# HGRN2's chunk states behind the last level in place of ahead of the diagonal, diagonal and levels two to three k-tiles sooner

## The reference

```python
def hgrn2_chunked(q, k, v, g, S0, chunk):
    """HGRN2: S_t = diag(f_t) S_{t-1} + k_t v_t^T with k_t = 1 - f_t, g = log f_t, o_t = S_t^T q_t."""
    def step(S, xs):
        qc, kc, vc, gc = xs
        b = jnp.cumsum(gc, axis=-2)
        diff = b[..., :, None, :] - b[..., None, :, :]
        decay = jnp.exp(jnp.where(incl, diff, -jnp.inf))
        A = jnp.einsum('bhtk,bhsk,bhtsk->bhts', qc, kc, decay)
        o = (jnp.einsum('bhck,bhkv->bhcv', qc * jnp.exp(b), S)
             + jnp.einsum('bhts,bhsv->bhtv', A, vc))
        bl = b[..., -1:, :]
        S_new = (jnp.exp(bl[..., 0, :])[..., None] * S
                 + jnp.einsum('bhck,bhcv->bhkv', kc * jnp.exp(bl - b), vc))
        return S_new, o
```

## Time and profile before

| | us |
|---|---|
| median of 3 runs | 3001.03 (2996.76 to 3002.65) |
| the profiled execution, its own time | 3001.41 |
| its span in the trace | 2999.7 |
| PE busy | 2924.2 (97% of the span) |
| DVE busy | 2022.4 (67%) |
| ACT busy | 1190.8 (40%) |
| PE in the chain that ended last | 90% |
| mean granted clock of PE | 0.992 |

### The profile page before, as it was taken

The page is one execution under the profiler, slowest core; times in us unless marked ns, Lnnn a source line. Parts: engine busy times, 40 slices in busy tenths (PEclk is TensorE's granted clock), DMA queues, the critical chain, the costliest instruction groups (busy, mean ns, idle before and its releaser), DMA issues.

```text
span 2999.7 us, 52045 instructions
## 1 busy us (share of the span) xinstructions
PE 2924.2 (97%) x21800; PEld 2876.1 (96%) x21800; DVE 2022.4 (67%) x2796; ACT 1190.8 (40%) x1506; POOL 316.7 (11%) x432
## 2 busy tenths in 40 slices
PE   7999999999999999999989999999999999999998
PEld 7999999999999999989989999999999999999998
DVE  5556564746464747465477777777778788788885
ACT  4333333333333333333244444444444444444454
POOL 5111102020201011102100000000000000000111
PEclk9999999999999999999999999999999999999999
DMA  7334573333233424345334444544567666666665
GB/s 215 68 84 77 78 78 72 82 79 79 64 92 59 100 49 96 87 126 148 109 108 139 155 146 139 162 139 146 159 202 225 195 193 193 197 192 196 193 196 185
DMA packets 516473, 397.46 MB, mean 133 GB/s; under 512 B 16960, under 2 KB 484176, under 8 KB 516240
## 3 DMA queue, kind: packets, MB, share of 16 engines
q1 hardware_dynamic: 462272, 268.86, 36.3%
q0 software_dynamic: 22896, 88.43, 8.0%
q10 hardware_dynamic: 31072, 36.85, 4.1%
HBM read 309.72 MB, written 84.37 MB: 131 GB/s over the span
## 4 chain that ended last, share of the span: by engine, by line
PE 90%; DVE 5%; issue 2%; ACT 2%; DMA 1%; ACTq 0%; POOL 0%; SPq 0%; DVEq 0%; POOLq 0%
PE main L1279 39%; PE main L936 32%; PE mx L1279 7%; PE mx L1179 2%; PE mx L1012 1%; PE mx L1076 1%; PE mx L1084 1%; PE mx L996 1%; DVE w_lo L1825 1%; PE mx L1119 0%; ACT w_hi L1367 0%; PE mx L1055 0%; PE mx L1186 0%; PE mx L1196 0%; ACT tmp L1458 0%
## 5 line engine op out<-in xcount | busy, mean ns | idle before, releaser
L1279 PE MATMUL main<-forms_b,w_hi 128*128 128x288 f32 x3072 | 616.6, 296 | 10.8 <-DVE w_lo L2371 6.6
L936 PE MATMUL main<-h_hi,w_hi 128*128 128x296 f32 (+1 forms) x2592 | 612.0, 317 | 12.0 <-DVE w_lo L1825 12.0
L1279 PE MATMUL main<-forms_a,w_hi 128*128 128x288 f32 x3072 | 615.4, 296 | 5.8 <-DVE forms_a L2424 4.7
L936 PE MATMUL main<-h_lo,w_hi 128*128 128x296 f32 (+1 forms) x2592 | 564.6, 299 | 0.0
L936 PE MATMUL main<-h_hi,w_lo 128*128 128x296 f32 (+1 forms) x2592 | 564.1, 299 | 0.0
L1279 PEld LDWEIGHTS main<-forms_b,w_hi 128*128 128x128 f32 x3072 | 494.3, 189 | 12.2 <-DVE w_lo L2371 9.4
L1279 PEld LDWEIGHTS main<-forms_a,w_hi 128*128 128x128 f32 x3072 | 495.0, 189 | 6.9 <-issue 5.2
L1279 PE MATMUL main<-forms_a,w_lo 128*128 128x288 f32 x1536 | 455.2, 296 | 0.0
L1279 PE MATMUL main<-forms_b,w_lo 128*128 128x288 f32 x1536 | 453.4, 295 | 0.0
L936 PEld LDWEIGHTS main<-h_hi,w_hi 128*128 128x128 f32 x2592 | 414.8, 191 | 27.8 <-DVE w_lo L1825 17.4
L936 PEld LDWEIGHTS main<-h_lo,w_hi 128*128 128x128 f32 x2592 | 422.1, 189 | 0.0
(11 more groups left out here) (381 smaller groups left out, 3583.3 us busy)
## 6 DMA issues: line engine op xcount, KB each, us to landing
w_raw<-in_w_in SPq DMA_DIRECT2D x130, 512.0 KB, 8.1
w_raw<-in_w_up SPq DMA_DIRECT2D x128, 512.0 KB, 4.2
w_raw<-in_w_down SPq DMA_DIRECT2D x100, 512.0 KB, 4.4
u_forms<-ub POOLq DMA_DIRECT2D x32, 1152.0 KB, 6.8
z<-x_scratch SPq DMA_DIRECT2D x32, 576.0 KB, 7.4
x_scratch<-z POOLq DMA_DIRECT2D x31, 576.0 KB, 3.1
stage<-u_forms ACTq DMA_DIRECT2D x30, 576.0 KB, 4.0
w_raw<-in_w_out SPq DMA_DIRECT2D x32, 512.0 KB, 4.0
```

The lines of the kernel that those rows point to most:

```text
L936: ins = mm(out[:, half, :], w[:, ring, k, :], x[:, kx, half * width:half * width + width], start=first and n == 0, stop=last_ and n == 2)
L1279: ins = mm(out, w[:, k, :], x[:, kx, :], start=i in (0, 1, 3) and k == 0 and n == 0, stop=k == KP - 1 and n == 2, skip_group_check=True)
```

## The change

The stage `stw` is put behind `l64`, and `diag` and the levels move up. The table becomes: `turn_k` 18, `diag` 20, levels 22, 25, 29, 32, 36, 40, 43, `stw` 47, `o` 50. The steps in `HG_PE` and `HG_DVE` follow; `stw` on PE now waits for `a64` as well, `diag` for `kdt`, the first two levels for ACT's copy `vt` in place of `sc_4` (they use the PSUM banks that it reads), and `o` for `sc_4` in place of `a64`. No operation is added or removed.

```diff
--- before.py
+++ after.py
@@ -196,8 +196,8 @@
               **spread(["t1"] + T_STEPS + ["p64", "tp64", "vn0", "st0"]
                        + [f"{s}_{c}" for c in range(1, NW) for s in ("ws", "vn", "st")], 25, 57),
               "stb": 58, "out": 61}
-HG_STAGES = {"gates": 0, "conv_in": 5, "gates_b": 8, "turn_v": 10, "turn_k": 18, "stw": 20, "diag": 22,
-             **spread([f"l{b}" for b in LEVELS] + ["o", "out", "st0"], 24, 58)}
+HG_STAGES = {"gates": 0, "conv_in": 5, "gates_b": 8, "turn_v": 10, "turn_k": 18, "diag": 20,
+             **spread([f"l{b}" for b in LEVELS] + ["stw", "o", "out", "st0"], 22, 58)}
 
 START_PE = ["conv_rows", "vec_rows"] + [f"turn{k}" for k in range(KT)] + ["rstd", "cols"]
 START_ACT = ["ln", "exp", "a", "lb", "b_exp", "b_ln", "b_sig", "s_exp", "s_ln", "e_exp"]
@@ -213,13 +213,12 @@
            + ["tt64", "vx0", "vx", "sc_0", "o0"] + [f"{s}_{c}" for c in range(1, NW) for s in ("r", "sc")]
            + ["sb", "y1", "y"])
 GDN_POOL = [f"x{b}" for b in INV]
-HG_PE = ["turn_v", "turn_k", "stw", "diag"] + [f"l{b}" for b in LEVELS] + ["o0", "o", "out", "st0"]
+HG_PE = ["turn_v", "turn_k", "diag"] + [f"l{b}" for b in LEVELS] + ["stw", "o0", "o", "out", "st0"]
 HG_ACT = (["exp", "zexp", "ln", "lnlb", "sig", "zln", "zsig", "eb", "kdexp", "vt"] + [f"e{b}" for b in LEVELS]
           + ["o0", "o", "osq", "oln", "oexp"])
 LEVEL_DVE = [s for i, b in enumerate(LEVELS[1:]) for s in ([f"a{LEVELS[i]}", f"q{b}", f"kk{b}"] + ([f"arg{2 * b}"] if b < 64 else []))]
-HG_DVE = (["clamp", "zclamp", "g", "b", "k0", "k", "kdarg", "kd", "arg1", "vx", "kdt", "q1", "arg2", "sc_0"]
-          + [f"sc_{c}" for c in range(1, NW)] + ["diag", "qe", "zs"] + LEVEL_DVE + ["a64"]
-          + ["y1", "y", "sb_scale", "sb"])
+HG_DVE = (["clamp", "zclamp", "g", "b", "k0", "k", "kdarg", "kd", "arg1", "vx", "kdt", "q1", "arg2", "diag", "qe", "zs"]
+          + LEVEL_DVE + ["a64"] + [f"sc_{c}" for c in range(NW)] + ["y1", "y", "sb_scale", "sb"])
 HG_POOL = ["zero"]
 
 
@@ -1160,11 +1159,13 @@
                     W(hdve, "kdt")
                     W(hdve, "vx")
                     W(hact, "vt")
+                    W(hdve, "a64")
                     mm(bank(0, 0, P), hkdt[:, 0, :], hvx[:, SB, :], start=True, stop=True)
                     for c in range(1, NW):
                         ins = mm(mxf[:, P * c:P * c + P], hkdt[:, c, :], hvt[:, c, :], start=True, stop=True)
                     hpe.done(ins, "stw")
                 elif stage == "diag":
+                    W(hdve, "kdt")
                     for c in range(NW):
                         ins = mm(mxf[:, 1024 + P * c:1024 + P * c + P], win(hk, c), win(hq, c), start=True, stop=True)
                     hpe.done(ins, "diag")
@@ -1172,14 +1173,17 @@
                     b = int(stage[1:])
                     i = LEVELS.index(b)
                     W(hdve, f"kk{b}" if i else "q1")
-                    W(hdve, "sc_4" if i < 2 else f"a{LEVELS[i - 2]}")
+                    if i < 2:
+                        W(hact, "vt")
+                    else:
+                        W(hdve, f"a{LEVELS[i - 2]}")
                     n_ = 64 if b == 64 else P
                     for c in t_levels(b):
                         left = win(hkk if i else hk, c, n_)
                         ins = mm(bank(i % 2, 64 * c, 64, n_), left, hqq[:, ctok(c):ctok(c) + 64], start=True, stop=True)
                     hpe.done(ins, stage)
                 elif stage == "o":
-                    W(hdve, "a64")
+                    W(hdve, "sc_4")
                     W(hact, "eb")
                     pe.wait_ge(s_hst, h * 16 + 16)
                     for b in range(SB):
```

## The result

The changed kernel takes 3072.82 us (median of 3 runs, 3069.53 to 3077.55) where the kernel before takes 3001.03: a ratio of 1.0247, with an interval of 1.0233 to 1.026. The forecast was 3058, with a range from 3034 to 3071. The direction, the two waits and their places are as forecast; what they cost beyond themselves is not. The profiled execution of the changed kernel is the slowest of its three; the mean clocks of the others were 0.982 (3069.53 us) and 0.981 (3072.82).

What follows compares the result with a forecast made beforehand. PE was taken to bound the kernel, busy 2924.2 of 2999.7 us. Terms 38.2 + 17.3 + 2.1 - 0.3 - 0.6 = +56.7 us on the profiled 3001.41 gave 3058 us, range 3034 to 3071.

Steps and rivals of the forecast that it cites:

- Two waits at levels 2 and 8: In each of seven stretches PE reaches both levels before DVE's operands: 2.5 and 2.95 us, together +38.2 us.
- No wait at levels 4, 16, 32 and 64: Level 4 stays with room; levels 16, 32 and 64 have an estimated 0.5 to 1.7 us to spare.
- none at `o` in the stretches: At `o`, three k-tiles behind the states' products, the operand chain has 0.4 us to spare.
- The states themselves cost nothing: The states' products take PE 1.12 us, as much at the new place as at the old.
- The last head: States' products directly ahead of `o`: PE waits, +2.1 us; its wait at level 4 loses some 0.3 us.
- The clock: Half clock behind each level 8 wait and every second level 2 wait, 1.65 us each: +17.3 us, bounds 0 and 23.
- rival (2): Every wait costs the clock, also the last head's: 3066 us, or 3069 with a further stretch wait; chance 0.14.
- the start: First head: two columns' turns of the DeltaNet gates move from k-tile 24 to 22: -0.6 us.
- The rule on the clock: Only idle gaps longer than both level waits lower the clock: clock term 0, 3041 us; as rival, chance 0.14.

Runs made afterwards that it cites:

- shorter waits: The changed kernel with level 2 one k-tile later (26) and level 8 two later (34; later levels 38, 41, 44): 3030.76 us, ratio 1.0109.

## Why the prediction was right and wrong

**Two waits at levels 2 and 8: right.** Forecast as idle time 2.35 and 2.8, found 2.33 and 2.80, in each of the seven stretches, at the two places named, with the causes named: DVE's wait for ACT at `w_lo`, forecast at about 2.5 us, is 2.45 at 879.84, and the border of units 3 and 4 for level 8. Filling both (3039.74) shows their price by itself: 38.7 us between the medians, and 5.4 us in each of the clean heads, where the step had 38.2 and 5.45.

**No wait at levels 4, 16, 32 and 64: right**, and none at `o` in the stretches. The total of line L1183 is 37.2 in 16, and 7 x 5.13 + 1.3 = 37.2.

**The states themselves cost nothing: right** (1.0005 with them alone moved).

**The last head: right.** The wait at `o` is 1.92 us, forecast as about 1.9; the one at level 4 is 0.81 where it was 1.02. Rows of the changed kernel:

```profile
1391.13 1.33 PE L1183 MATMUL mx<-tmp 128*128 128x64 f32 x10 [0.81 <-DVE tmp L2069]
...
1421.99 1.95 PE L1190 MATMUL mx<-tmp,hstate 128*128 128x8 f32 x16 [1.92 <-DVE tmp L2137]
```

**The clock: the step that failed.** "I let each of its seven cost the clock ... I count every second. 7 x 1.5 x 1.65 = +17.3 us. The bounds are 0 and 14 x 1.65 = 23 us." Two things were wrong in it. In the changed kernel not every second but every wait of 2.33 us cost clock, so that 14 of 14 did; that is what rival (2) had. And one spell of about 3.3 us per wait, taken from one place of the MLP, was half of what followed: 6.8 us at 13 of them. The price of a piece was about right: 1.50 and 1.56 us in two experiments, against 1.65. In the profiled execution the term is 27 x 1.52 = 41 us, and between the medians, by the kernel with filled gaps, 33: both beyond the bound of 23. The windows from level 2 to level 2, of after and of before, show it in one row each: PE's busy time in the same 1151 or 1148 records is 159.82 against 153.22 us, and the clock 0.96 against 1.00.

```profile
882.61:1049.88 167.27, 159.82 (x1151) 154.68 (x1151) 90.50 (x162) 54.13 (x76) 21.10 (x28) 0.96 0.32 72
```

```profile
843.00:998.87 155.87, 153.22 (x1148) 148.22 (x1148) 89.78 (x161) 54.27 (x76) 20.86 (x28) 1.00 0.34 77
```

The row in the MLP was one sample of a thing that varies with its position, and I used it as a price. The trace of before had the longer spell too, at the last head's wait for `w_lo`:

```profile
1363.24 0.85 PE L936 MATMUL main<-h_hi,w_hi 128*128 128x288 f32 x2 [4.31 <-DVE w_lo L1825]
```

```profile
1361.00:1367.70 6.70, 4.46 (x18) 4.46 (x19) 3.98 (x5) 0.00 (x0) 1.05 (x2) 0.50 0.37 102
```

The prediction passed over it: it reads the 9s in the earlier trace rows as the full level in every slice. Two other terms partly covered the miss: the start was 2.1 us better where I had 0.6, and 2.4 us of small waits went that I had not counted.

**The range** had its top at 3071, 1.8 us below the result. It followed from "14 x 1.65", with an allowance for one more wait, and no allowance for a longer spell.

**The rule on the clock.** The forecast kept a rule of the Trainium skill as a rival. What the runs show: in the changed kernel all waits of 2.80 and 2.33 us came with a granted clock of 0.50, in the kernel with the levels alone 13 of 14, and so did five of seven of 1.51 us. The Trainium skill (TensorE: Matmul & The Clock Gate, HAM oscillation) has as its rule that only idle gaps longer than any of these do harm; by it this kernel would have taken 3041, as the forecast worked out, and the measurement decides against it. The same section tells of a kernel in which the loss is paid anew in each turn of the loop; with that this trace agrees, with 6.8 us behind both waits in six heads one after the other.

## What to carry to other kernels

In an order written by hand, an operation's place on the engine that uses it is only half of the change: read where its operand stands in the making engine's own queue, above all whether a wait for a third engine (here the rounding of weights) stands ahead of it. Where the operand can be made ahead of that, the earlier place costs nothing; the same look at the waits already in the table then gave 0.66%. Price a new wait of a nearly always busy PE at its length plus a loss of clock that can be as large again (here 38 and 41 us for the waits of 2.33 and 2.80 us; 1.5 us or nothing behind those of 1.51), and let the range reach from the loss in no turn to the longest spell in every turn: one wait of 14 in a kernel like this one cost no clock, and the wait of 1.51 us cost it in five heads and not in two.

## What the runs showed of the hardware

- The half clock came in pieces of 3.4 or 6.8 us here, and 3.4 us of it cost 1.50 (158.97 against 160.47) to 1.56 us (161.17 against 162.73). Which of the two followed went with how long after the wait the clock fell: 6.8 us where it fell from 0.5 us ahead of the wait's end to 0.4 behind it, 3.4 where it fell 0.6 to 2.1 us behind. That is what the seven stretches of five kernels have in common (changed, levels alone, level 8 alone, level 2 alone, shorter waits); the last head does not keep to it (before, a fall at 1296.1, 0.04 us behind a wait of 3.39, lasted 3.4), and no experiment moved the one against the other.
- A wait of 1.51 us was enough in five heads and not in two of the same kernel, and 1.87 us in the MLP was not. Nor was one of 2.33 us in the sixth stretch of the kernel with the levels alone. Why the same wait did it in one head and not in another is not settled; both heads have the same work ahead of the wait.
- Work of no use was cheaper here than no work: 15 and 18 matmuls in the gaps of each stretch took the kernel from 3072.8 to 3039.7 us.
- The two periods of one loop, with the shorter and the longer spell, can alternate in one execution (161.17, 162.73, 161.13, 162.74 us from the first diagonal to the fifth, with level 8 alone early); the changed kernel settled on one from its second head on.
